# Fused Mamba and cache-attention stage: convolution parts between the pairs of sample states, and ScalarE's output copy ahead of the next decays

## What is computed

```python
# per layer: project x to q, k, v, forget logits, z, xBC, dt and two gates, then
xbc, new_buf = causal_conv(xbc, conv_buf, conv_w, conv_b)    # 4 taps along time, then silu
xs, bm, cm = jnp.split(xbc, [D_SSM, D_SSM + SSM_GROUPS * SSM_STATE], axis=-1)
y, h_new = ssd(xs, dt, a, bm, cm, h0)                        # chunks of 128 tokens, 8 groups
y = (y + d_skip * xs) * silu(z)                              # then a root-mean-square norm per group

# the samples attend over 2048 cached positions, held in pages of 128
lg_past = einsum('bqhd,bkhd->bhqk', q, k_past) * scale + cn + rev
p = softmax(concatenate([lg_past, lg_new]))
out = einsum('bhqk,bkhd->bqhd', p[..., :past], v_past) + einsum(..., p[..., past:], v)
```

## Time and profile before

| what | us |
|---|---|
| median of 3 runs | 6265.98 |
| lowest and highest of them | 6254.58 and 6267.96 |
| the profiled execution | 6227.53 |
| its span, first to last instruction | 6225.8 |
| busy in the span: PE, DVE, POOL, ACT | 4570.9, 3199.9, 1635.4, 686.3 |
| one full round of the fused stage | 126 to 127 |

### The profile page before, as it was taken

One profiled execution on the slowest core, in us unless ns is written; L12 is line 12 of the kernel. 1 busy time (PEld: TensorE's weight loads), 2 busy tenths in 40 slices (PEclk: granted clock), 3 DMA queues, 4 the chain that ended last, 5 costly groups with the idle time before them and its releaser, 6 DMA issues. The chain is left out here.

```text
span 6225.8 us, 58980 instructions
## 1 busy us (share of the span) xinstructions
PE 4570.9 (73%) x22581; PEld 3456.5 (56%) x22581; DVE 3199.9 (51%) x4356; ACT 686.3 (11%) x992; POOL 1635.4 (26%) x1698
## 2 busy tenths in 40 slices
PE   8999999969688878889688699989899990000000
PEld 8999999955455656567433585555555550000000
DVE  2222222225455545400011218878888978998888
ACT  2111111113111111100000110000000000000000
POOL 0000000000343343200000001222222227777775
PEclk9999999985688888889899899999999995555555
DMA  4323232321455565442411328999999998999998
GB/s 151 110 105 110 104 110 106 109 64 41 139 195 178 177 206 173 153 152 95 186 54 47 112 79 343 419 418 404 419 421 421 421 421 346 410 394 395 370 387 336
DMA packets 337237, 1444.78 MB, mean 232 GB/s; under 512 B 87929, under 2 KB 126889, under 8 KB 198689
## 3 DMA queue, kind: packets, MB, share of 16 engines
q0 software_dynamic: 176880, 990.49, 40.7%
q1 hardware_dynamic: 141792, 427.53, 19.0%
q10 hardware_dynamic: 18432, 25.17, 1.1%
HBM read 1345.37 MB, written 99.47 MB: 232 GB/s over the span
## 5 line engine op out<-in xcount | busy, mean ns | idle before, releaser
L1985 DVE SCALAR_TENSOR_TENSOR i_acc<-i_row,i_cf,i_acc 128x2048 f32<-128x2048 f32 x571 | 1344.8, 2355 | 202.8 <-DMA i_row<-in_expert_v,i_ei 143.3
L1792 PE MATMUL i_p_h<-i_xT,i_ut 128*128 128x384 f32 x4096 | 1329.7, 488 | 37.7 <-DMA i_ut<-in_u_tiles 30.2
L1792 PEld LDWEIGHTS i_p_h<-i_xT,i_ut 128*128 128x128 f32 x4096 | 781.2, 191 | 583.8 <-DMA i_ut<-in_u_tiles 31.4
L2101 POOL DMA_INDIRECT i_row<-in_expert_v,i_ei x576 | 578.3, 1004 | 628.2 <-DVE i_acc L1985 469.6
L199 PE MATMUL a_acc<-a_xh,a_wh 128*128 128x288 f32 x3104 | 654.0, 292 | 25.3 <-DVE a_wl L254 25.3
L199 PE MATMUL a_acc<-a_xh,a_wl 128*128 128x288 f32 x3104 | 653.7, 292 | 0.0
L199 PE MATMUL a_acc<-a_xl,a_wh 128*128 128x288 f32 x3104 | 653.7, 292 | 0.0
L199 PEld LDWEIGHTS a_acc<-a_xh,a_wh 128*128 128x128 f32 x3104 | 494.0, 188 | 25.3 <-DVE a_wl L254 25.3
L199 PEld LDWEIGHTS a_acc<-a_xl,a_wh 128*128 128x128 f32 x3104 | 493.8, 188 | 0.0
L199 PEld LDWEIGHTS a_acc<-a_xh,a_wl 128*128 128x128 f32 x3104 | 493.8, 188 | 0.0
L1976 DVE CUSTOM_DVE_ANT_0 i_row<-i_row,i_acc 128x2048 f32<-128x2048 f32 x192 | 432.0, 2285 | 107.1 <-DMA i_row<-in_expert_u,i_ei 104.9
(11 more groups left out here) (277 smaller groups left out, 4734.4 us busy)
## 6 DMA issues: line engine op xcount, KB each, us to landing
i_ut<-in_u_tiles SPq DMA_DIRECT2D x128, 1024.0 KB
a_w<-in_w_in SPq DMA_DIRECT2D x97, 1024.0 KB, 4.8
tmp_uT<-a_out POOLq DMA_DIRECT2D x97, 288.0 KB, 2.4
tmp_Ha<-i_ho ACTq DMA_DIRECT2D x128, 192.0 KB
f_ws<-in_w_bs SPq DMA_DIRECT2D x16, 1024.0 KB, 6.8
g_wo<-in_w_out SPq DMA_DIRECT2D x4, 4096.0 KB, 29.8
h_w<-in_w_query SPq DMA_DIRECT2D x16, 1024.0 KB, 5.0
c_csb<-tmp_cs SPq DMA_DIRECT2D x32, 288.0 KB
```

The lines of the kernel that those rows point to most:

```text
L1792: last = nc.tensor.matmul(p_h[:, e % 2, 0:ND], ut[:, e % 4, k * P:(k + 1) * P], xT[:, k, :], start=(k == 0), stop=(k == KT - 1))
L1985: v.scalar_tensor_tensor(acc, row[:, m % R, :], cf[:, j, k:k + 1], acc, ALU.mult, ALU.add).then_inc(row_used, 1)
L2101: pool.indirect_dma_start(row[:, m % R, :], None, table, bass.IndirectOffsetOnAxis(index, axis=0)).then_inc(row_in[m % R], 16)
```

## The change

On VectorE, part 3 of the next group's convolution is computed ahead of the first pair of sample states, part 0 between the first pair and the second, and only part 1 is left behind `gated`. On ScalarE the copy of the attention output goes ahead of the next group's decays. TensorE, GpSimd and SyncE keep their lists. Nothing is added or taken away.

```diff
                     after_matrix(g, 4)
-                    for u in range(4):
+                    if g < 7:
+                        conv(g + 1, 3)
+                    for u in range(2):
+                        sample_states(g, u)
+                    if g < 7:
+                        conv(g + 1, 0)
+                    for u in range(2, 4):
                         sample_states(g, u)
                     gated(g)
                     if g < 7:
-                        for a in (3, 0, 1):
-                            conv(g + 1, a)
+                        conv(g + 1, 1)
                     mean_square(g)
                     outputs(g)
...
                     if g < 7:
                         conv(g + 1)
-                        decays(g + 1)
                     act.wait_ge(l_out, g + 1)
                     act.wait_ge(o_out, g + 1)
                     nc.scalar.mul(ov[:, :], e_ps[:, 0:2, :]..., st[:, 11:12]).then_inc(oc_out, 1)
+                    if g < 7:
+                        decays(g + 1)
                     act.wait_ge(n_free, g + 1)
                     nc.scalar.activation(ms[:, :], ms[:, :], ACT.Sqrt).then_inc(root_out, 1)
```

## The result

| | before | with the change |
|---|---|---|
| median of 4 runs, us | 6264.09 | 6157.51 |
| lowest and highest | 6254.58, 6267.96 | 6142.85, 6180.36 |
| ratio to before, 95% interval | | 0.9835 [0.9802, 0.9869] |
| span of the profiled execution | 6225.8 | 6161.3 |
| fused stage, first `new_scores` to last `turn_out` | 985.5 | 898.9 |

The change makes the kernel 107 us faster; the interval reaches from 82 to 124 us. The forecast of 6184 us lies 26 us above the median and inside its range. The profiled spans differ by less, 64.5 us, since the execution that was profiled before was 37 us quicker than the median of its kernel and the other one 6 us slower than its own. The fused stage itself is 86.6 us shorter, but it began 23.5 us later in the second profile (1667.1 against 1643.6), since the input projection ahead of it was slower there. Experiments 3 and 8 show whose difference that is.

The account below looks back on a forecast made before the run. TensorE's wait in `turn_out` for ScalarE's copy was taken as the bound. 73 us of pause plus 9 us of clock made 82 us, so 6266 − 82 = 6184 us, range 6156 to 6214.

Parts of the forecast that it names:

- What bounds the kernel: Fused stage: TensorE's `turn_out` waits for ScalarE's copy, 80.3 us in 7 waits, behind late convolution parts and the decays.
- The pause: 73 us: TensorE's wait ahead of `turn_out` shrinks from 11.43 to about 1.05 us a round, in seven rounds.
- Cover for the two moved parts: Parts 3 and 0, 3.74 us each, fit VectorE's idle 8.30 and 12.59 us; cost nothing, 4.6 and 8.8 to spare.
- The decays behind the copy: ScalarE's next-group decays, now after the copy, cost nothing; if the slack were gone, up to 3 us a round.
- The clock: 9 us: TensorE behind `turn_out`: faster transposes and a third of `new_scores` give 1.3 us a round, clock still falling.
- The rival of the clock that stays up (6170 us): TensorE's clock does not fall behind `turn_out`: 3.3 us a round, 23 us beside the pause's 73; chance 0.27.
- The rival of the pages: Next round's key-page waits grow as TensorE arrives earlier, taking up to half the gain: 6225 us, chance 0.07.
- Held-up gathers, the slower rival: Convolutions delay GpSimd's page gathers: 6485 us, chance 0.03; gathers standing for all of part 3: 6210 us, chance 0.08.
- The sum: Whole kernel: 73 + 9 = 82 us off the median of 6266 us, giving 6184 us.
- signs of being wrong: Copy wait above 3 us, its return as a wait for key or value pages, or later rounds shorter than 112 us.

Follow-up runs that it names:

- run 3: The changed kernel, unaltered, timed and profiled again on another set's chip: 6166.7 us, ratio 0.9847 to the kernel before.
- run 8: The kernel before, unaltered, profiled again on the chip with shorter stages: 6115.0 us, stage 886.9 us.
- Run 1: Against the kernel before, only VectorE's half: parts 3 and 0 between the sample states, ScalarE's copy left behind the decays; 6207.5 us, ratio 0.9929.
- run 2: Against the kernel before, only ScalarE's half: the copy ahead of the decays, VectorE as before; 6242.0 us, ratio 0.998.
- run 9: The changed kernel, unaltered, as the control of the last set: 6153.6 us against 6253.5, ratio 0.9849.
- sets A and C: Two of the three sets of follow-up runs, each on its own chip beside the kernel before; the changed kernel's ratios were 0.9847 and 0.9849.
- set B: The set of follow-up runs on the chip with shorter stages, the only one with a profile of the kernel before, which took 6115.0 us.
- run 6: Against the changed kernel, part 3 moved behind the first pair of sample states, so parts 3 and 0 stand between the pairs; ratio 0.984.
- Run 5: Against the changed kernel, the 16 multiplies of `new_scores` done twice into the same place; stage 827.9 us, whole time not given.

## Why the prediction was right, and where it was off

- **What bounds the kernel.** Right. The wait for ScalarE's copy, made of three late convolution parts and the decays ahead of it, was the price. Run 1 and run 2 have its two shares, 3.93 and 8.41 us left, against 11.43 − 7.49 = 3.94 and 11.43 − 2.89 = 8.54. What the prediction didn't see is the second largest idle time, the 58.2 us in small pieces among the scores.
- **The pause: 73 us.** Measured 80.3 − 6.8 = 73.5. Right.
- **Cover for the two moved parts.** Right in that both had cover, but the size of the second was taken from the wrong round. Round 1's 12.59 us ahead of the third sample states is the longest of the seven, since TensorE had waited 4.36 us for a value page there; the others have 7.2 to 9.5. With the change 3.3 to 7.1 us are left. In round 1 the idle time fell by 3.1 and 6.2 us and not by 3.7 each, since that round's page wait was 2.97 us in the second profile and the multiplies behind it took 8.80 us, not 9.68.
- **The decays behind the copy.** Right: no row of the waits has VectorE waiting for them. In round 1 of the profile after, the load of the exponential's table starts the instant the copy ends.
- **The clock: 9 us. This is the mis-sized term.** The head gave 26.1 us in the first profile, 20 and 23 in runs 3 and 9 against that profile's before. Two things failed. The rate of `new_scores` at full clock was taken from L946's 5.09 us, a row that was partly slow itself: at full clock 16 such multiplies take 1.78 us and not 2.5, so a head without a fall gains 4.0 us and not 3.3. And the fall was expected in every round; it came in 6 of 21. Where it came, the gain was 14.9 − 14.0 = 0.9 us, near the 1.3 forecast.
- **The rival of the clock that stays up (6170 us)** described the first profile better. That its 23 us were about right in size is partly luck: it also used the 2.5 us for `new_scores`, and with 1.78 it would have been 4.0 us a round, 28 us, of which the one fall took 3.2.
- **The rival of the pages.** Its mechanism is not what the rows show. It read the idle time among the scores as a wait for key pages, but in these pieces TensorE waited for nothing that the profile shows. Something of its size did appear, and the sum had nothing for it: keys and values took 13.7 us more in the first profile, where that idle time grew by 10 us and the value-page waits by 3.4. But against the same before they took 10.4 us more in run 3 and nothing more in run 9, and the sets A and C have no profile of the kernel before. On the chip of set B, where that idle time is 0, keys took 247.4 us in runs 6 and 8 alike and values 4.0 us more. So it stays open whether the change costs anything there or the profiles only differ.
- **Held-up gathers, the slower rival.** Did not happen. The six key gathers of round 1 took 0.94 us each but one. Part 3 ran from 1863.38 to 1867.26, and these are the three that fell beside it:

```profile
1863.24 0.94 POOL L604 DMA_INDIRECT e_kr<-in_cache_k,e_ik  x1 [0.30 <-issue]
1864.48 1.35 POOL L604 DMA_INDIRECT e_kr<-in_cache_k,e_ik  x1 [0.30 <-issue]
1866.14 0.94 POOL L604 DMA_INDIRECT e_kr<-in_cache_k,e_ik  x1 [0.30 <-issue]
```

  By the rule of the Trainium skill (the page "SBUF — State Buffer", section "Who interferes with whom") a gather that comes while VectorE runs an instruction with two SBUF inputs waits until that instruction has ended. The trace agrees beside the scan of 4.41 us, where a gather took 4.84 us in the profile after too, and roughly for the gather of 1.35 us, which came 0.55 us before the end of such an instruction. Each of part 3's six such instructions is short, 0.28 or 0.75 us, and the gathers go on between them: all the gathers beside it were delayed by 0.4 us together. What failed is the rival's step from single instructions to all 3.74 us of the part. In run 6, with part 3 elsewhere, the value pages' waits were no shorter.
- **The sum.** 82 us forecast. By its own terms it should have been 73.5 + 26 − 14 = 86 for the stage, which is what the stage shows. The two errors, 17 us too little for the clock and 14 too much by leaving out what keys and values took more, nearly cancelled, and that is luck. The same luck is in the rounds: the six full ones took 113.2 to 117.4 us, 114.9 on average, inside the 114 to 115 forecast for a falling clock, though the clock fell in one of them only. None of the prediction's signs of being wrong came up, for none of them was shorter than 112 us. The medians moved by 107, 85 and 100 us (first runs, sets A and C), each with an interval of some 20 us to either side, so they can't tell 82 from 86.

## What to carry to other kernels

When a wait is named, follow the waited-for engine back through its own list: here the instruction that TensorE wanted was short and ready, and what stood ahead of it on its engine had no hurry. Such a pause was also paid in TensorE's clock here, and that part came back only when the pause was almost gone: taking away two thirds of it (run 1) returned none. Read a cover from several rounds, not from one. And when a price at full clock is needed, check the granted clock of the very row it is read from.

## What was not expected of the hardware

- With a pause of 0.92 us ahead of `turn_out` and `new_scores` the clock fell in some rounds and not in others of one execution: 10.9 or 14.0 us for the same instructions. Without the pause it never happened in 28 rounds. What picks the rounds was not found.
- In run 6 it was lost in six of seven rounds with the same pause. Run 5, on the same chip with part 3 in its usual place, had lost it in five of seven before anything in it differed from the changed kernel. So it speaks for the chip and not for the place of part 3, though the changed kernel itself was not run there.
- The input projection runs at 292 or 295 ns a matmul from one execution to the next, 31 us of the span, in both kernels. A difference of spans between two profiles has to be read stage by stage.
- The same kernel took 6115 us on one chip and 6252 on another. Of the two profiles of it, 86 us of the difference are in the keys' part of the fused stage (247.4 against 333.6 us in seven rounds), where one has idle time among the multiplies that no wait explains and the other none; 38 us more lie behind the stage.
